# Three passes instead of two finish their rows directly, and the final tiles are read one pass sooner

## The reference, cut to what matters

```python
x = x + _hier_moe(h, ...)        # per token: sum over its 2 experts of
                                 # coef * (silu(h @ w_gate) * (h @ w_up)) @ w_down
return x * rsqrt(mean(x * x, -1) + EPS) * final_g
```

## Time and profile before

| | us |
|---|---|
| median of 3 runs | 1061.48 (1059.52 to 1061.57) |
| the profiled execution, own time | 1065.91 |
| its span in the trace | 1063.8 |
| TensorE busy in it | 992.4 (93%) |
| DVE busy | 488.4 (46%) |
| ACT busy | 276.6 (26%) |
| GpSimd busy | 150.1 (14%) |

### The profile page before, as it was taken

One profiled execution on the slowest core, in us unless ns is written; L12 is line 12 of the kernel. 1 busy time (PEld: TensorE's weight loads), 2 busy tenths in 40 slices (PEclk: granted clock), 3 DMA queues, 4 the chain that ended last, 5 costly groups with the idle time before them and its releaser, 6 DMA issues. The chain is left out here.

```text
span 1063.8 us, 13459 instructions
## 1 busy us (share of the span) xinstructions
PE 992.4 (93%) x5091; PEld 579.0 (54%) x5091; DVE 488.4 (46%) x1221; ACT 276.6 (26%) x621; POOL 150.1 (14%) x146
## 2 busy tenths in 40 slices
PE   6999999999999899999999999996999969899991
PEld 4435787666555566666766555564454324344440
DVE  3495490396546277666664224273741211111115
ACT  3201111302223576566654101020100101001024
POOL 4000000130211221110011000011122102202230
PEclk9999999999999899999999999986999989989996
DMA  9400240223200650000000233455899999999955
GB/s 256 126 30 4 79 79 0 27 19 115 65 1 1 141 184 2 1 2 1 1 2 1 99 139 134 183 200 215 293 320 384 383 405 396 392 392 397 368 185 213
DMA packets 61744, 165.79 MB, mean 156 GB/s; under 512 B 32747, under 2 KB 34859, under 8 KB 49319
## 3 DMA queue, kind: packets, MB, share of 16 engines
q1 hardware_dynamic: 53296, 145.99, 38.5%
q0 software_dynamic: 8096, 18.42, 6.8%
q10 hardware_dynamic: 288, 0.53, 0.1%
HBM read 147.41 MB, written 25.24 MB: 162 GB/s over the span
## 5 line engine op out<-in xcount | busy, mean ns | idle before, releaser
L2015 PE MATMUL banks<-shared,wout 128*128 128x512 f32 (+1 forms) x368 | 146.1, 609 | 12.0 <-issue 10.3
L1616 PE MATMUL banks<-wout,shared 128*128 128x512 f32 x256 | 112.7, 594 | 0.5 <-PEq L1276 0.5
L2015 PEld LDWEIGHTS banks<-shared,wout 128*128 128x128 f32 (+1 forms) x368 | 56.2, 172 | 84.4 <-issue 84.0
L1324 ACT ACTIVATE shared<-shared,low 128x640 f32<-128x640 f32 (+7 forms) x128 | 92.9, 729 | 3.0 <-DVE low L1411 2.5
L2063 DVE SCALAR_TENSOR_TENSOR mix_bt<-mix_bt,slot_coef,banks 128x256 f32<-128x256 f32 x24 | 11.5, 481 | 168.7 <-ACT mix_bt L2043 168.5
L385 PE MATMUL banks<-x,wout 128*128 128x512 f32 x192 | 84.6, 595 | 0.8 <-DVE x L426 0.8
L1374 PE MATMUL banks<-consts,shared 128*128 128x128 f32 x528 | 79.2, 286 | 2.1 <-ACT shared L1324 1.3
L1374 PEld LDWEIGHTS banks<-consts,shared 128*128 128x128 f32 x528 | 56.9, 142 | 41.8 <-issue 36.9
L1616 PEld LDWEIGHTS banks<-wout,shared 128*128 128x128 f32 x256 | 47.6, 190 | 55.2 <-issue 55.2
L2037 PE MATMUL banks<-shared,hidt 128*128 128x512 f32 (+1 forms) x184 | 72.6, 596 | 1.9 <-DVE wout L2078 1.3
L1356 PE MATMUL banks<-shared 64*128 64x512 f32 (+3 forms) x384 | 72.0, 493 | 1.9 <-PEq L995 1.3
(11 more groups left out here) (366 smaller groups left out, 1346.2 us busy)
## 6 DMA issues: line engine op xcount, KB each, us to landing
shared<-in_exp_w_down SPq DMA_DIRECT2D x23, 1024.0 KB, 25.3
shared<-in_exp_w_gate SPq DMA_DIRECT2D x23, 1024.0 KB, 15.0
shared<-in_exp_w_up SPq DMA_DIRECT2D x23, 1024.0 KB, 22.7
x<-in_exp_w_down SPq DMA_DIRECT2D x9, 1024.0 KB, 29.6
x<-in_exp_w_gate SPq DMA_DIRECT2D x5, 1024.0 KB, 20.2
x<-in_exp_w_up SPq DMA_DIRECT2D x5, 1024.0 KB, 30.1
wout<-in_w_in SPq DMA_DIRECT2D x16, 256.0 KB, 5.2
wout<-in_w_in SPq DMA_DIRECT2D x2, 2048.0 KB, 8.0
```

What stands on the lines that cost most here:

```text
L1324: nc.scalar.activation(prob[:, u % 2, at:at + n], prob[:, u % 2, at:at + n], ACT.Exp, bias=low[:, u % 2, v, j:j + 1], scale=-1.0, accum_ou ...
L1616: ins = nc.tensor.matmul(psum[n % 4], src[:, i * P:i * P + P], m["wout"][:, k, half * 512:half * 512 + 512], start=k == 0, stop=k == KD - 1)
L2015: ins = nc.tensor.matmul(psum[2 + p][rows].rearrange("p (a f) -> p a f", a=2), xt[:, p, k, rows], wgu[b][:, :, k], start=k == 0, stop=k == ...
```

## The change

`DIRECT` becomes 3: passes 21, 22 and 23 finish their rows directly (`first` = 21). What follows from it, and what is changed beside it:

- SP's tile loads wait for the scatter of pass 20, not 21.
- Passes 21 and 23 serve experts of the same half, so a token may be in both. GpSimd therefore writes the sums of pass 21 back to `x_rows` with a plain scatter (`put_rows`), after all tile loads have landed, then gathers the residual rows of pass 23; and the indirect store of pass 23 to `out` waits until that of pass 21 has landed.
- `shared_tiles` become 0, 1, 4 and 7; `store_order` becomes 2, 3, 0, 1, 5, 6, 4, 7.
- The roots are taken in four groups: tiles 0 to 3 with pass 21; tiles 4 to 7; pass 22; pass 23.
- TensorE keeps its overlapped order to the end, and the down products of pass 23 go to banks 0 and 1.

```diff
@@ -45,7 +45,7 @@
...
 LISTS_AT = 3
-DIRECT = 2
+DIRECT = 3
 DUMMY = T
@@ -1944,15 +1944,15 @@
...
     assert all(buffer_of(j) not in (0, 5) for n in range(first, NP) for j in passes[n][1])
-    assert not any(passes[n][2] & passes[n - 1][2] for n in range(first - 1, NP))
+    assert not any(passes[n][2] & passes[n - 1][2] for n in range(first, NP))
     homes = ([wgu[0].rearrange("p a k f -> p (a k f)")[:, i * D:i * D + D] for i in range(4)]
              + [wd[0][:, i] for i in range(2)] + [m["spare"][:, i * D:i * D + D] for i in range(2)])
-    by_square = [("x", i) for i in range(NT)] + [("z", i) for i in range(DIRECT)]
-    by_norm = [("x", i) for i in range(2, NT)] + [("z", i) for i in range(DIRECT)]
-    shared_tiles = (0, 1)
-    store_order = (2, 3, 4, 0, 5, 1, 6, 7)
+    by_square = [("x", i) for i in range(4)] + [("z", 0)] + [("x", i) for i in range(4, NT)] + [("z", 1), ("z", 2)]
+    by_norm = [("x", 2), ("x", 3), ("z", 0), ("x", 5), ("x", 6), ("z", 1), ("z", 2)]
+    shared_tiles = (0, 1, 4, 7)
+    store_order = (2, 3, 0, 1, 5, 6, 4, 7)
     gained, scaled = sem("rows_gained"), sem("rows_scaled")
-    groups = [slice(0, 4), slice(4, 8), slice(8, 10)]
+    groups = [slice(0, 5), slice(5, 9), slice(9, 10), slice(10, 11)]
     nth_norm = {what: k + 1 for k, what in enumerate(by_norm)}
@@ -1972,6 +1972,9 @@
...
 
+    def residual_landed(eng, n):
+        eng.wait_ge(x_in[n % UN], 16 * gathered[n] + 16)
+
     def residual_rows(gp, n):
@@ -1989,12 +1992,17 @@
...
         gp.wait_ge(out_stored, 16 * NT)
+        if i >= 2:
+            out_landed(gp, i - 2)
         nc.gpsimd.indirect_dma_start(out[0], bass.IndirectOffsetOnAxis(m["tok"][:, passes[n][0]:passes[n][0] + 1], 0),
...
         eng.wait_ge(x_in[n % UN], 16 * gathered[n] + 32)
+
+    def y_bank(n):
+        return 0 if n == NP - 1 else 6
 
@@ -2024,7 +2032,7 @@
...
 
-    def pe_down(pe, n, bufs, p, wait):
+    def pe_down(pe, n, bufs, p, wait, bank=6):
         pe.wait_ge(s["h_out"], n + 1)
@@ -2034,7 +2042,7 @@
...
                     rows = slice(v * w, v * w + w)
-                    ins = nc.tensor.matmul(psum[6 + part][rows], hidt[:, p, k, rows], wd[b][:, k, part * 512:part * 512 + 512],
+                    ins = nc.tensor.matmul(psum[bank + part][rows], hidt[:, p, k, rows], wd[b][:, k, part * 512:part * 512 + 512],
                                            start=k == 0, stop=k == 1)
@@ -2075,7 +2083,7 @@
...
             cols = slice(part * 512, part * 512 + 512)
-            V.tensor_tensor(y[:, n % 2, cols], xg[:, n % UN, cols], psum[6 + part], ALU.add).then_inc(s[done], 1)
+            V.tensor_tensor(y[:, n % 2, cols], xg[:, n % UN, cols], psum[y_bank(n) + part], ALU.add).then_inc(s[done], 1)
 
@@ -2160,7 +2168,7 @@
...
                 if i in shared_tiles:
-                    sp.wait_ge(scaled, i - shared_tiles[0] + 1)
+                    sp.wait_ge(scaled, shared_tiles.index(i) + 1)
                 else:
@@ -2197,19 +2205,30 @@
...
                     scatter(gp, n - 1)
-                if n >= first:
+                if first <= n < first + 2:
                     residual_rows(gp, n)
-            gp.wait_ge(fg_in, 16)
-            for i in shared_tiles:
+
+            def gained_tile(i):
                 gp.wait_ge(ss_done, column["x", i].stop)
                 nc.gpsimd.tensor_tensor(homes[i], homes[i], m["fg"], ALU.mult).then_inc(gained, 1)
+
+            gp.wait_ge(fg_in, 16)
+            for i in shared_tiles[0:2]:
+                gained_tile(i)
+            for tile_in, landed in last_in:
+                gp.wait_ge(tile_in, landed)
+            residual_landed(gp, first + 1)
+            put_rows(gp, first)
+            gained_tile(shared_tiles[2])
+            residual_rows(gp, first + 2)
+            gained_tile(shared_tiles[3])
             for i in range(DIRECT):
...
                     out_landed(gp, i)
-                for n in range(first, NP):
+                for n in range(first + 1, NP):
                     put_rows(gp, n)
@@ -2239,28 +2258,38 @@
...
                 act.wait_ge(o_done, nth_norm[known])
-                act.wait_ge(gained, i - shared_tiles[0] + 1)
+                act.wait_ge(gained, shared_tiles.index(i) + 1)
                 nc.scalar.mul(homes[i], homes[i], rstd[:, column["x", i]]).then_inc(scaled, 1)
+
+            def roots(g):
+                act_roots(act, groups[g], groups[g].stop)
 
...
                 act_hid(act, n, n % 2)
+            act_gate(act, first, first % 2)
             act_y(act, first - 1, (first - 1) % 2, rows_out(first - 1))
-            act_gate(act, first, first % 2)
-            squares((0,))
+            act_hid(act, first, first % 2)
             act_gate(act, first + 1, (first + 1) % 2)
-            act_hid(act, first, first % 2)
-            squares((1, 2, 3))
+            squares((0, 1))
             act_hid(act, first + 1, (first + 1) % 2)
-            act_roots(act, groups[0], 4)
-            squares((4, 5, 6, 7))
-            act_roots(act, groups[1], 8)
-            squares((8, 9))
-            act_roots(act, groups[2], 10)
-            for i in shared_tiles:
+            squares((2, 3, 4))
+            roots(0)
+            squares((5, 6))
+            act_gate(act, first + 2, (first + 2) % 2)
+            act_hid(act, first + 2, (first + 2) % 2)
+            squares((7, 8))
+            roots(1)
+            for i in shared_tiles[0:2]:
                 scaled_tile(i, ("x", 2))
+            squares((9,))
+            roots(2)
+            for i in shared_tiles[2:]:
+                scaled_tile(i, ("x", 5))
+            squares((10,))
+            roots(3)
 
@@ -2301,24 +2330,19 @@
...
                     pe.wait_ge(wd_in[buffer_of(j)], 16 * nth[j])
-                pe_down(pe, n, [buffer_of(j) for j in passes[n][1]], n % 2, n > 0)
-
-            for n in range(first):
+                pe_down(pe, n, [buffer_of(j) for j in passes[n][1]], n % 2, 0 < n < NP - 1, y_bank(n))
+
+            for n in range(NP):
                 up(n)
-                next_x(n + 1)
+                if n + 1 < NP:
+                    next_x(n + 1)
                 if n:
...
                     slots()
-            next_x(first + 1)
-            down(first - 1)
-            up(first)
-            up(first + 1)
-            for n in range(first, NP):
-                pe_hid(pe, n, n % 2)
-                down(n)
+            down(NP - 1)
 
@@ -2469,22 +2493,26 @@
...
                     some(5)
+            dve_hid(dve, first, passes[first][0], first % 2)
             dve_x(dve, first + 1, (first + 1) % 2)
             dve_y(dve, first - 1, (first - 1) % 2, rows_out(first - 1))
-            for n in range(first, NP):
-                dve_hid(dve, n, passes[n][0], n % 2)
+            dve_hid(dve, first + 1, passes[first + 1][0], (first + 1) % 2)
+            dve_x(dve, first + 2, (first + 2) % 2)
             dve.wait_ge(fg_in, 16)
...
             inverses(0)
-            for i in (2, 3):
-                dve_scaled(("x", i))
+            for what in by_norm[0:3]:
+                dve_scaled(what)
+            dve_hid(dve, first + 2, passes[first + 2][0], (first + 2) % 2)
             dve_sum(dve, first + 1)
             inverses(1)
-            for i in (4, 5, 6, 7):
-                dve_scaled(("x", i))
+            for what in by_norm[3:5]:
+                dve_scaled(what)
+            dve_sum(dve, first + 2)
             inverses(2)
-            for i in range(DIRECT):
-                dve_scaled(("z", i))
+            dve_scaled(("z", 1))
+            inverses(3)
+            dve_scaled(("z", 2))
 
```

More of the change, by code:

```diff
@@ L2272, in all_again @@
                     act_square(act, ("x", i), NT + DIRECT + i, 1)
-                act_roots(act, slice(0, NT), NT + DIRECT + NT)
+                act_roots(act, slice(groups[0].start, groups[1].stop), NT + DIRECT + NT)
             tiles_over(act, over_tile, None, all_again)
@@ L2495, in all_again @@
                 dve.wait_ge(root_done, len(groups) + 1)
-                for h in range(2):
-                    four = slice(4 * h, 4 * h + 4)
-                    inverse_root(nc, chain, rstd[:, four], root[:, four], ss[:, four], newton)
+                for g in groups[0:2]:
+                    inverse_root(nc, chain, rstd[:, g], root[:, g], ss[:, g], newton)
                 for i in range(NT):
```

## The result

The change makes the kernel slower: ratio to the kernel before 1.0045, 95% interval 1.0025 to 1.0066, some +4.8 us; medians 1067.43 and 1061.53 of six runs each. The profiled execution of the change has a span of 1067.6 where that of before has 1063.8. On the median of before that the prediction started from, 1061.48, the ratio gives 1066.3: at the upper end of its range (1059.2 to 1066.8), 2.9 above the time forecast.

What follows compares the result with a forecast made beforehand. The prediction took the landing of all tiles, set by the third tile store's issue plus 9.1 us, and the closing stores as the bound. −0.45 and +2.3 gave +1.9 on 1061.5, so 1063.4 us, range 1059.2 to 1066.8.

Steps and rivals of the forecast that it cites:

- the lead: Tile loads wait for pass 20's scatter instead of pass 21's, so all tiles land 4.6 us sooner; ACT's order loses most.
- the third store: Pass 23's indirect store to `out` waits until the first has landed and is not hidden: 2.3 us more, at most 2.8.
- L: The moment when the eight tiles of `out` have landed; forecast at 1055.6, with −0.45 us as its term in the sum.
- rival A: GpSimd's multiply of tile 4 holds VectorE's third scaling, delaying pass 23 and the third tile store: +4.3 us, chance 0.25.
- Tile loads: SP issues them 6.2 us after pass 20's scatter, at 1022.5 instead of 1027.18; all landings come 4.6 us sooner.
- rival C: The gather for pass 21 delays the scatter's landing by 1 to 2 us: +2.9 to +3.9, chance 0.08.
- the second root: On ACT, after tiles 6 and 7 and a third root table load; its multiply of tile 0 then ends at 1046.4.
- The step that failed: On GpSimd, the plain scatter ahead would push tile 4's multiply past DVE's third scaling, where it hurts nobody.
- L as the issue of the third tile store plus 9.1: The last six tile stores run as one stream, ending 9.1 us after the first of them is issued.
- From L to the end: The closing stores to `out` grow from L + 5.4 to L + 7.7, or 8.2 with the longer restart: +2.3 us.
- Rival B: The lead carries through to ACT's second root, the third store moves 4.6 us: end 2.3 sooner, 1059.2, chance 0.10.
- D: Nothing to be seen: the third indirect store lands in under 3.3 us, ACT idles under 1.7; +0.5 or so, chance 0.12.

Runs made afterwards that it cites:

- e5: The change, with only ACT's gate of pass 23 moved ahead of the first root; ratio to the kernel before 1.0026.
- e3: The change, with pass 23's gate ahead of the first root on ACT and its product ahead of the first inverse root on VectorE; ratio to the kernel before 1.0012.
- e6: The change, with tiles 4 and 7 scaled by VectorE again, GpSimd multiplying only tiles 0 and 1; ratio to the kernel before 1.0040.
- e7: The edits of e3 and e6 together on the change; ratio to the kernel before 1.0024.
- e4: The change, with pass 23's indirect store to the output left out; ratio to the kernel before 1.0024.
- e1: The change, with GpSimd's multiply of tile 4 moved behind the gather of pass 23's residual rows; ratio to the kernel before 1.0033.
- e8: The kernel before, with tiles 0, 1, 4 and 7 shared by GpSimd and ACT, still two direct passes; ratio to the kernel before 1.0026.
- e2: The change, with VectorE forming pass 23's product ahead of its third scaling; ratio to the kernel before 1.0036.
- e10: The kernel before, with ACT multiplying tiles 0 and 1 right behind the second root and these stored third and fourth; ratio to the kernel before 0.9982.
- e9: e7, with VectorE scaling pass 22's rows ahead of the sum of pass 23; ratio to the kernel before 1.0000.

## Why the prediction came out as it did

The direction stands, and so do the two causes that it named: the lead is lost in ACT's and DVE's orders, and the third store is not hidden. The size it forecast as likeliest (+1.9) was too small, and its term for L had the wrong sign: −0.45 forecast, +1.95 measured. What happened is rival A, priced at +4.3 and given 0.25, with +4.8 measured.

- **Tile loads:** 6.03 after the scatter (6.2 expected), 4.88 sooner. The new gather for pass 21 didn't delay them: rival C falls.
- **ACT and the lost lead:** three table loads of 1.28, nothing between load and neighbours, as forecast. The drain that the Trainium skill, "ScalarE: Activation LUTs", section "What ACT_TABLE_LOAD costs", adds isn't seen: the load at 1036.12 ends at 1037.40 and the gate starts at 1037.42, and the load that e5 saves ahead of the second root is worth 1.29. The forecast put the second root at 28.6 us from the scatter (1044.9), and it came at 30.66, 2.06 later. The held scaling makes 2.08 of that; the first root came 0.4 sooner than forecast, and from DVE's product to ACT's next square the change took 1.53 where the forecast had 1.2. TensorE's two transposes between them took 0.70, at a granted clock of 0.50; where TensorE wasn't idle ahead of them they took 0.39, at 1.00 (e3). (The forecast's own sum from the copy to the multiply of tile 0 is off by 0.2: its terms give 1046.2, not 1046.4.)
- **The step that failed** is the argument against A, that "the plain scatter just ahead would so push the multiply past DVE's third scaling". The scatter took 1.02, and the multiply followed 0.02 us behind it, 0.18 before DVE's third scaling; the forecast had put it between 0.1 before and 0.3 behind. The scaling took 2.08 us more, and with it went product, copy and root. A longer scatter would not have saved it either. In all nine runs with the plain scatter its issue ended 2.16 to 2.20 us after the start of DVE's first scaling, whether it took 1.01 (e6), 1.80 (e5) or 1.91 (e7): it began during that scaling and ended some 0.9 after it. So wherever the multiply stood right behind it and the third scaling behind the second, it came 0.18 to 0.19 ahead of the third (change, e3, e4, e5). A scatter that begins during the second scaling wasn't tried. e1, e6 and e8 show the hold as the cause, e2 that it counts through pass 23's product. This agrees with the exclusive lock that the Trainium skill, "SBUF — State Buffer", section "SBUF: two separate sides", states.
- **L as the issue of the third tile store plus 9.1:** in the change that store is issued at 1047.24 and L is 9.72 later; in e10 9.12 (the store 1.53 sooner than in before, L 1.52 sooner); in e7, beside the gather for pass 23, 11.27 (1039.18 to 1050.45). The rule moved L rightly in e10 and is too short by 0.6 in the change and 2.2 in e7. In e7 the new gather shares the stream. In the change it doesn't: the DMA engines move nothing from 1046.5 to 1048, and then 402 GB/s to 1055.5, as before (404). What makes the last landing 0.6 later there stays open. So the +1.95 of L is 1.34 from the third tile store and 0.6 from this; that rival A's price for L (−0.45 + 2.4) is the same +1.95 is in part luck.
- **From L to the end:** +2.9, not +2.3. The restart after the landing took 0.79 (1061.11 to 1061.90), where the forecast took 0.3 and kept 0.82 for the upper end.
- Sum by the measured terms: L +1.95 and the serial store +2.9 give +4.85.
- **Rival B** was tried by e3 and e7: with the order repaired and the late multiplies gone the lead comes through as far as the second root (3.5 of 4.9 us), and L is 2.9 sooner; the serial store takes just that. **D** fell: the third store lands in the same 3.3 us, and ACT idles 4.30, not less than 1.7.

## What to carry to other kernels

Move elementwise work from VectorE to GpSimd only where VectorE has no scaling, scan or small step of an inverse root to do meanwhile; near the end of a chain a 2.3 us multiply on GpSimd held one of these for about as long (a scaling by 2.08), and moving it only moved the hold, while beside sums from PSUM it cost nothing. When loads are made earlier, look for the first engine whose written order mixes the new early work with the old late work: here one gate and one product sat behind squares and scalings and gave the whole lead back. And count waits that stand one behind the other at the very end at their full latency, since nothing there hides them.

## What was unexpected

- A DVE operation of 4 columns waited through two GpSimd multiplies in a row (4.12 us, e1); in the earlier stage scans and multiplies took turns.
- It works in the other direction too: in e7 four of GpSimd's indirect issues took 1.50 to 1.91 us in place of 1.0. Each began during a DVE scaling of 1.28 and ended 0.87 to 0.89 after that scaling's end. The plain scatter of the change, at 1.02, looks free of it only because it began 0.10 before a scaling's end. In e9 the first store's issue began with no scaling running, and took 1.00.
- DVE's sums, with one input in PSUM, weren't held: in e7 two of them took their usual 1.28 from 1023.59 on, while GpSimd's multiplies began at 1024.15 and took their usual 4.68 for two.
- TensorE's last down products took 6.38 us for 8 matmuls, against 3.67. The engine had been idle for 5.70 us ahead of them. The windows of the change around them (start and end, length, busy time of TensorE, its weight load, DVE, ACT and GpSimd, then the granted clock as a share of full speed, the DMA share and GB/s):

```profile
1036.00:1040.00 4.00, 0.00 (x0) 0.00 (x0) 4.00 (x3) 1.77 (x4) 3.48 (x2) 0.73 0.65 259
1040.00:1042.00 2.00, 0.63 (x2) 0.31 (x2) 2.00 (x4) 0.00 (x0) 0.00 (x0) 0.50 0.39 154
1042.00:1046.00 4.00, 3.45 (x5) 1.51 (x5) 0.51 (x1) 3.86 (x7) 2.38 (x2) 0.50 0.24 66
1046.00:1049.00 3.00, 3.00 (x5) 0.97 (x3) 2.62 (x7) 3.00 (x4) 0.99 (x1) 0.65 0.34 137
```

The clock was granted at 0.50 while they began, the 1.2 GHz level of the two (1.2 and 2.4 GHz), and at 0.65 on average over the last window; in the kernel before it stayed at 1.00 through the same products. For the down products it cost nothing here, since they ended at 1049.01 and DVE came to the sum of pass 23 only at 1050.33. The two transposes ahead of them, 0.70 in place of 0.39, lie on the way to the second root: about 0.3 us.
